# Seven-product block multiplications: three products move onto the first product's banks, and its kept copy is added to one quadrant

## What is computed

```
x      = x + merged @ w_out                    # first block: "out",  512x1024 by 1024x1024
hid    = silu(hn @ w_ffn_gate) * (hn @ w_ffn_up)
x      = x + hid @ w_ffn_down                  # first block: "prod0", "prod1", and a plain rest
...
x      = x + y @ w_o                           # second block: "wo",  512x1024 by 1024x1024
return rmsnorm(x, final_g)
```

## Time and profile before

| | us |
|---|---|
| median of 3 runs | 1255.16 (1254.71 to 1255.23) |
| time of the profiled execution | 1255.48 |
| its span in the profile | 1253.7 |
| TensorE busy | 1238.8 (99%) |
| VectorE busy | 819.1 (65%) |
| ScalarE busy | 559.5 (45%) |
| "out" on TensorE | 345.4 to 385.5 |
| "prod0" on TensorE | 485.7 to 524.0 |
| "prod1" on TensorE | 611.2 to 649.7 |
| "wo" on TensorE | 1206.9 to 1246.2 |

### The profile page before, as it was taken

How to read it: one execution, slowest core, us unless ns; L and a number is a source line. 1 busy time by engine, 2 the same in 40 slices (tenths; PEclk the granted TensorE clock), 3 DMA queues, 4 the chain that set the end, 5 groups by cost and what they waited for, 6 DMA issues and landing times.

```text
span 1253.7 us, 15550 instructions
## 1 busy us (share of the span) xinstructions
PE 1238.8 (99%) x6018; PEld 1040.4 (83%) x6018; DVE 819.1 (65%) x1280; ACT 559.5 (45%) x966; POOL 146.9 (12%) x208
## 2 busy tenths in 40 slices
PE   9999999999999999999999999999999999999997
PEld 8878888888888888888888888888898888888885
DVE  6885667745697555665665579858875436436687
ACT  5456564653455333333332263438764343223344
POOL 0002341221000100100000000005550000000200
PEclk9999999999999999999999999999999999999999
DMA  6242323129564943783432233321116332332971
GB/s 200 68 108 68 84 77 93 51 85 235 185 168 165 240 133 101 229 207 101 101 127 92 86 94 111 117 81 34 35 35 201 101 92 77 104 99 87 235 174 75
DMA packets 119509, 149.03 MB, mean 119 GB/s; under 512 B 14406, under 2 KB 90252, under 8 KB 119436
## 3 DMA queue, kind: packets, MB, share of 16 engines
q1 hardware_dynamic: 105868, 115.53, 29.0%
q0 software_dynamic: 13552, 32.51, 11.9%
q10 hardware_dynamic: 16, 0.00, 0.0%
HBM read 142.78 MB, written 2.10 MB: 116 GB/s over the span
## 4 chain that ended last, share of the span: by engine, by line
PE 90%; DVE 5%; ACT 2%; issue 1%; POOL 1%; DVEq 0%; ACTq 0%; POOLq 0%
PE ps_mm L2473 60%; PE ps_mm L2508 9%; PE ps_s L2784 3%; PE ps_mm L2784 3%; PE ps_t L2784 2%; PE ps_o L2784 2%; PE ps_s L2629 1%; PE ps_o L2929 1%; DVE w_lo L1520 1%; PE ps_o L2673 1%; PE ps_mm L2548 1%; PE ps_t L2916 1%; PE ps_s L2695 1%; PE ps_t L2653 1%; ACT w_hi L908 1%
## 5 line engine op out<-in xcount | busy, mean ns | idle before, releaser
L2473 PE MATMUL ps_mm<-act_hi,w_hi 128*128 128x512 f32 x944 | 372.0, 394 | 0.3 <-DVE w_lo L1520 0.3
L2473 PE MATMUL ps_mm<-act_hi,w_lo 128*128 128x512 f32 x944 | 370.0, 392 | 0.0
L2473 PE MATMUL ps_mm<-act_lo,w_hi 128*128 128x512 f32 x944 | 369.7, 392 | 0.0
L1520 DVE TENSOR_TENSOR w_lo<-stage,w_hi 128x2048 fp32r<-128x2048 f32 (+5 forms) x98 | 205.2, 2094 | 125.2 <-ACT w_hi L908 125.0
L908 ACT ACTIVATE w_hi<-stage 128x2048 fp32r<-128x2048 f32 (+5 forms) x99 | 171.9, 1736 | 150.9 <-PE ps_mm L2473 72.1
L2473 PEld LDWEIGHTS ps_mm<-act_hi,w_lo 128*128 128x128 f32 x944 | 177.4, 188 | 35.8
L2473 PEld LDWEIGHTS ps_mm<-act_hi,w_hi 128*128 128x128 f32 x944 | 177.4, 188 | 35.3 <-DVE w_lo L1520 0.8
L2473 PEld LDWEIGHTS ps_mm<-act_lo,w_hi 128*128 128x128 f32 x944 | 177.5, 188 | 34.7
L2508 PE MATMUL ps_mm<-w_hi,act_hi 128*128 128x512 f32 (+2 forms) x144 | 52.7, 366 | 0.6 <-DVE lat L1661 0.5
L2508 PE MATMUL ps_mm<-w_lo,act_hi 128*128 128x512 f32 (+2 forms) x144 | 52.2, 362 | 0.0
L2508 PE MATMUL ps_mm<-w_hi,act_lo 128*128 128x512 f32 (+2 forms) x144 | 52.2, 362 | 0.0
(11 more groups left out here) (519 smaller groups left out, 2364.9 us busy)
## 6 DMA issues: line engine op xcount, KB each, us to landing
stage<-in_w_in SPq DMA_DIRECT2D x43, 1024.0 KB, 5.3
sums<-in_w_ffn_down POOLq DMA_DIRECT2D x16, 1024.0 KB, 9.5
stage<-in_w_ffn_gate SPq DMA_DIRECT2D x11, 1024.0 KB, 5.7
stage<-in_w_ffn_up SPq DMA_DIRECT2D x11, 1024.0 KB, 7.4
stage<-in_w_ffn_down SPq DMA_DIRECT2D x8, 1024.0 KB, 5.1
osum<-in_w_out POOLq DMA_DIRECT2D x6, 1024.0 KB, 8.7
tsum<-in_w_o POOLq DMA_DIRECT2D x6, 1024.0 KB, 8.4
stage<-in_w_out SPq DMA_DIRECT2D x4, 1024.0 KB, 5.1
```

What stands on the lines that cost most here:

```text
L1520: V.tensor_tensor(w_lo[:, s, 0:k * w], raw, w_hi[:, s, 0:k * w].bitcast(F32), ALU.subtract).then_inc(w_lo_made, 1)
L2473: ins = T.matmul(ps_mm[:, 2 * bank_slot + m, :], wt[:, kk, m * P:(m + 1) * P], acts[ap][:, kk, :], start=(r == 0), stop=(r == per - 1), sk ...
```

## The change

P6, P7 and P4 now add in place to P1, on P1's pair of banks, and P2, P5 and P3 use the other pair: P2 opens it, P5 opens it anew, P3 adds to P5. The banks then hold P1, P1+P6, P1+P6+P7, P1+P6+P7+P4 in turn, so what `keep_product` adds to the other quadrants already has P1 in it, and the kept copy is added in the upper left alone. `spread` with its three calls becomes `add_first` with one. P6 now waits for `p1_kept`, and P2 no longer does. In "prod1" P1 waits for P4's banks of "prod0" and P2 for P3's. The numbering of the bank pairs of the later units is turned (`pair_of`).

```diff
--- before.py
+++ after.py
@@ -174,7 +174,7 @@
 
 def pair_of(g):
 
-    return (g + (g >= GROUP[U0["ffn"]])) % 2
+    return g % 2
 
 
 def group_of(u):
@@ -419,8 +419,8 @@
         def half_bank(n, p, j):
 
             if n == "out":
-                return ps_mm[:, 2 * ((GROUP[U0["ffn"]] + (p in ("P6", "P7", "P4"))) % 2) + j, :]
-            return (ps_t, ps_o)[j][:, :] if p in ("P6", "P7", "P4") else ps_s[:, j, :]
+                return ps_mm[:, 2 * ((GROUP[U0["ffn"]] + (p in ("P2", "P5", "P3"))) % 2) + j, :]
+            return ps_s[:, j, :] if p in ("P2", "P5", "P3") else (ps_t, ps_o)[j][:, :]
 
         def side_bank(k):
             return (ps_s[:, 0, :], ps_s[:, 1, :], ps_t[:, :], ps_o[:, :])[k % 4]
@@ -1948,10 +1948,9 @@
                     else:
                         V.tensor_tensor(r, half_bank(n, p, j), r, ALU.add).then_inc(product_kept, 1)
 
-            def spread(p1, tt, cc, op):
-
-                link(V.tensor_tensor(res[:, tt, cc], res[:, tt, cc], p1[:, :, :], op))
-                after(chain[0])
+            def add_first(p1):
+
+                after(link(V.tensor_tensor(res[:, 0:2, left], res[:, 0:2, left], p1[:, :, :], ALU.add)))
 
             for i in range(1, 4):
                 lo(GATE_B[i] + 1)
@@ -1967,7 +1966,7 @@
                         merge_lo(2 * i - 2 + m)
                     merged_sums(i - 1)
             uo, uf = U0["out"], U0["ffn"]
-            right, left, up, down = slice(512, D), slice(0, 512), slice(0, 2), slice(2, 4)
+            right, left = slice(512, D), slice(0, 512)
             merge(4)
             merge(5)
             merge_lo(4)
@@ -1986,17 +1985,14 @@
             lo(uo + 3)
             dve.wait_ge(res_landed, 16 * TT)
             keep_product("out", "P6")
+            dve.wait_ge(p1_kept, 2)
+            add_first(p1_m)
             keep_product("out", "P2")
             lo(uo + 4)
-            dve.wait_ge(p1_kept, 2)
-            spread(p1_m, down, left, ALU.add)
             keep_product("out", "P7")
             lo(uo + 5)
-            dve.wait_ge(product_kept, kept_at("out", "P7") + 2)
-            spread(p1_m, down, right, ALU.subtract)
             keep_product("out", "P5")
             lo(uo + 6)
-            spread(p1_m, up, right, ALU.subtract)
             keep_product("out", "P4")
             lo(uf)
             keep_product("out", "P3", (0,))
@@ -2017,10 +2013,7 @@
 
                 dve.wait_ge(p1_kept, 2 * GROUPS + 2)
                 dve.wait_ge(product_kept, 12 * GROUPS + 12)
-                right, left = slice(512, D), slice(0, 512)
-                for tt, cc, op in ((slice(0, 2), right, ALU.subtract), (slice(2, 4), right, ALU.subtract),
-                                   (slice(2, 4), left, ALU.add)):
-                    link(V.tensor_tensor(res[:, tt, cc], res[:, tt, cc], xacc[:, :, :], op))
+                link(V.tensor_tensor(res[:, 0:2, 0:512], res[:, 0:2, 0:512], xacc[:, :, :], ALU.add))
                 after(chain[0])
 
             def operands(j):
@@ -2394,15 +2387,12 @@
 
             u = U0["wo"]
             keep_product("wo", "P6")
+            lo(u + 3)
             dve.wait_ge(p1_kept, 2 * GROUPS + 4)
-            spread(p1_y, down, left, ALU.add)
-            lo(u + 3)
+            add_first(p1_y)
             keep_product("wo", "P2")
-            spread(p1_y, down, right, ALU.subtract)
             lo(u + 4)
             keep_product("wo", "P7")
-            dve.wait_ge(product_kept, kept_at("wo", "P6") + 2)
-            spread(p1_y, up, right, ALU.subtract)
             lo(u + 5)
             keep_product("wo", "P5")
             dve.wait_ge(fg_landed, 16)
@@ -2765,16 +2755,16 @@
                 for j, ks in parts:
                     if j and between is not None:
                         between()
-                    if n == "out" and p in ("P1", "P6") and ks[0] == 0:
+                    if n == "out" and p in ("P1", "P2") and ks[0] == 0:
                         g = GROUP[uf0] - (2 if p == "P1" else 1)
                         pe.wait_ge(bank_free, dve_freed(g, j))
-                    if p == "P2":
+                    if p == "P6":
                         pe.wait_ge(p1_kept, 2 * GROUPED.index(n) + j + 1)
                     elif p in ("P7", "P5", "P4", "P3"):
                         pe.wait_ge(product_kept, kept_at(n, {"P7": "P6", "P5": "P2", "P4": "P7", "P3": "P5"}[p]) + j + 1)
                     elif n == "prod1":
-                        pe.wait_ge(product_kept, kept_at("prod0", "P3" if p == "P1" else "P4") + j + 1)
-                    opens = p in ("P1", "P6", "P5")
+                        pe.wait_ge(product_kept, kept_at("prod0", "P4" if p == "P1" else "P3") + j + 1)
+                    opens = p in ("P1", "P2", "P5")
                     for kk in ks:
                         if n in ("out", "wo") and p in ("P1", "P2"):
                             pe.wait_ge(chunk_lo_made, (MERGED_AT + MERGED_LO.index(2 * kk + (p == "P2")) if n == "out" else Y_AT + 2 * kk + (p == "P2")) + 1)
```

## The result

The changed kernel took 1257.14 us (median, 1256.29 to 1258.06), the kernel before in the same comparison 1255.20: a ratio of 1.0015 with an interval of [1.0008, 1.0022], that is 1.9 us more, between 1.0 and 2.8. The forecast was 1256.9, or 1.8 us more. The work taken from VectorE is gone, and it bought nothing.

The account below looks back on a forecast made before the run. TensorE, busy 99%, was taken to bound the kernel, so VectorE's relief counted as nothing. Waits of 0.89 ("wo"), 0.59 ("prod1") and 0.30 ("out") sum to 1.78 us on 1255.16, giving 1256.9; range 1255.0 to 1258.4.

Parts of the forecast that it names:

- "out": In "out" the addition now precedes P5's low part, so P5 starts 0.18 us late, with a restart +0.30 us.
- "prod1": In "prod1" P6 waits for VectorE's sum of P1's first half, made behind P6's low part: +0.59 us.
- "wo": In "wo" P6 waits for ScalarE's copy of P1's first half, late behind a table load: +0.89 us.
- What was removed: Six additions on VectorE in "out", "wo" and behind the FFN products, 7.3 us, costed at nothing on the path.
- Adding in place and turned banks: Adding onto P1 instead of opening a bank, and turned banks and pairs in later units, taken as 0 us.
- VectorE's relief: Rival: the seven microseconds taken from VectorE shorten TensorE's waits, 1254.8 us without new waits at P6; chance 0.04.
- The hidden waits: Rival: P6 finds P1's copy already made, or the tail makes up the time, giving 1255.2 us; chance 0.06.
- The late low part in "out": Rival: P5's late start pushes each following low part, losing 0.3 us four times, 1257.8 us; chance 0.08.
- The clock: Rival: the longer wait ahead of P6 in "wo" drops TensorE from 2.4 to 1.2 GHz, 1262.4 us; chance 0.03.
- the estimate of 1.3 us more: In "wo", by the skill's 2.66 us table switch, P6 would be 2.1 us late, not 0.89; not used.
- The waits of P6: Profile sign: about 0.9 to 1.1 us in "wo" ending with L1181, near 0.8 us in "prod1" ending with L1939.
- the second copy: In "wo" P1's second half is copied by 1215.66, before P6's second half at 1216.3: no second wait.

Follow-up runs that it names:

- e4: The kernel before with six of its nine additions of P1's kept copy left out, nothing else; 1255.11 us, ratio 0.9999.
- e7: Changed kernel, "out" addition behind P5's low part, both "wo" copies early, high parts ahead of second Silu (FFN) and P5's second square ("wo"); 1253.58 us.
- e8: The kernel before with only e7's two turned ScalarE orders (high part ahead of second Silu, and of P5's second square in "wo"); 1253.52 us, ratio 0.9986.
- e6: Changed kernel with e2's and e5's moves, plus the "out" addition put back behind P5's low part; 1255.51 us, ratio 1.0001.
- e2: Changed kernel with VectorE's addition of P1's first half in "prod1" moved ahead of P6's low part; 1256.56 us, ratio 1.0011.
- e1: Changed kernel with ScalarE's copy of P1's first half in "wo" moved ahead of the square root and its table load; 1256.39 us, ratio 1.0010.
- e5: On top of e1, ScalarE's copy of P1's second half in "wo" also moved ahead of P2's high part; 1256.27 us, ratio 1.0007.

## Why the prediction was right

- **The sum.** Forecast +1.78 us, measured +1.94 in the medians and +1.81 from "out" to the end. By places, taken at the fourth matmul of the product, where the restart is over: "out" +0.29 (forecast 0.30), "prod0" 0 (0), "prod1" +0.62 (0.59), "wo" +0.91 (0.89). Each came from a subtraction of rows of the trace before. Two small errors nearly cancel: the matmul starts 0.1 us behind the copy and not 0.05, and the restart of TensorE costs 0.09 us behind the two long gaps and not 0.12. The span went up by 2.5 us and not by the forecast 1.8, because "out" happened to start 0.6 us later in that execution. The prediction also has P6 0.2 us late before the change in three places; that is so in "wo", and in the two FFN products it was 0.3 (a gap of 0.53 us), which none of its sums uses.
- **What was removed is worth nothing.** Forecast from 125.0 of 125.2 us in the earlier trace rows; e4 shows it alone, and e7 against e8 shows it where TensorE waits least.
- **Adding in place and turned banks cost nothing.** e6 leaves 0.08 us for them together, which the noise covers.
- **The rivals.** VectorE's relief is refuted by e4. The hidden waits are refuted by the timelines. The late low part in "out" did not run on: the next one waits for ScalarE again, and "out" lost 0.3 us once. The clock did not fall behind the longer gap: P6's matmuls in "wo" start 0.23 us apart from the second on (1215.31, 1215.54, 1215.78), the pace of the higher level, 2.4 GHz. But the prediction's ground for expecting this did not hold. Its wait of 2.1 us is the stretch ahead of TensorE's first matmul, and the matmuls behind it ran at the pace of the lower level, 1.2 GHz, whatever says (last section). In the kernel before the longest time between two matmul starts at the higher level was 0.93 us, so nothing in that trace spoke for 1.39. That this rival got only a small chance and did not come was luck and not a reading. The table load was again followed by the next ScalarE instruction within 0.01 us of its end and by the copy 0.12 us later, with the 1.28 us of the load alone; the 2.66 us that the Trainium skill gives for a switch ("ScalarE: Activation LUTs", What ACT_TABLE_LOAD costs) do not show in this trace, and the estimate of 1.3 us more did not come.
- **What I said the profile would show and did not.** The waits of P6 do not end with L1181 and L1939 in the list but with L1520. The times are right and the name is not; a reader who trusted the name would have tried to make the low part earlier. e2's rival (a low part moved later makes it worse) is that reading, and the gap of 0.65 us refutes it.
- **What I had not seen.** In "wo" I cleared the second copy only for the case of a late first half. e1 shows that it is 0.3 us late otherwise; and the slack of P2's low part that I took for a microsecond in e5 was 0.12 us.

## What to carry to other kernels

Where an engine is at 99%, the value of a change is in the waits of that engine alone: list them first, and count work taken from another engine as nothing until one of them ends with it. The exception is the tail behind its last matmul, where the other engines set the time (0.4 us in e8). A change that reuses an accumulator moves a wait to an earlier instruction; subtract the end of the copy from the start of the instruction that now waits, at every place and for every half, and look which instruction stands ahead of the copy on its engine (here a table load, and a low part). The gain was in ScalarE's order: three times a high part stood behind one activation that was itself waiting for another engine. Putting it ahead gave 1.56 us at TensorE's gaps and 0.4 in the tail.

## What was unexpected about the hardware

Executions start at two paces. The first matmuls of 128x384 start 0.32 us apart and later ones 0.17, and the step between them comes at another time in each program, here in the timeline of the kernel before and of e1:

```profile
11.63 0.52 PE L2548 MATMUL ps_mm<-w_hi,act_hi 128*128 128x384 f32 x1
11.96 0.46 PE L2548 MATMUL ps_mm<-w_hi,act_lo 128*128 128x384 f32 x1
12.25 0.34 PE L2548 MATMUL ps_mm<-w_lo,act_hi 128*128 128x384 f32 x1
12.43 0.34 PE L2548 MATMUL ps_mm<-w_hi,act_hi 128*128 128x384 f32 x1
```

```profile
10.99 0.44 PE L2538 MATMUL ps_mm<-w_hi,act_lo 128*128 128x384 f32 x1
11.27 0.33 PE L2538 MATMUL ps_mm<-w_lo,act_hi 128*128 128x384 f32 x1
11.44 0.34 PE L2538 MATMUL ps_mm<-w_hi,act_hi 128*128 128x384 f32 x1
```

By their pace these are the two levels, 1.2 and 2.4 GHz: 384 columns in 0.32 us are 1.2 columns a nanosecond. The full pace came at about 12.3 us before, 12.6 in the changed kernel and 11.2 in e1. The windows over 10 to 12 us report a granted clock of 1.00 in each. That is no measurement: the traces' own record of the granted clock begins at 12.2, 12.6 and 11.2 us, just at the step, and time without a record is counted as 1.00. So the 1.00 over the first 5 us in the earlier trace rows says nothing either, and the spacing of the matmuls is what to read. The Trainium skill has the rule ("TensorE: Matmul & The Clock Gate", What you observe and What's actually happening): the default is throttled, activity releases it, and the moment varies from run to run. The traces agree that the lower level comes first and that the moment varies: over the ten programs, one execution each, the record begins between 10.4 and 13.4 us. That activity is what releases it, no run here tests. From the matmul at about 26 us on, the ten programs take 319.3 to 319.7 us to the first matmul of "out". So most of the reason why "out" starts between 344.8 and 346.4 us, in programs that are the same up to there, lies ahead of 26 us: in this step and in the landing of the first loads (the 0.8 us at L1610 in the changed kernel's list of waits). Whether it also makes the whole spread of the medians' runs was not tried.

A restart of TensorE costs about 0.1 us beyond the wait: the first matmul behind a gap takes 0.47 to 0.50 us in place of 0.39, and the second starts 0.31 to 0.34 behind it instead of 0.23. By the fourth matmul that is 0.12 to 0.14 us behind gaps of 0.39 to 0.83 us, and 0.09 behind the two of 1.18 and 1.39 us. It is paid once for each gap, so a wait of 0.16 us in "out" cost 0.29.
